# The shared expert's down product moved from the end of the expert loop into its turns, and the second norm's vectors loaded as single rows

## The reference, cut to what matters

```
for i in range(2):
    tok, q_mem = fox_mix(...) if i % 2 == 0 else rwkv7_mix(...)
    mixed = concatenate([tok, memory_cross_attention(q_mem, ...)]) @ w_out[i]
    x = layer_norm(DEEPNORM_ALPHA * x + mixed, ln1_g[i], ln1_b[i])
    ffn = moe_ffn(x, ...)
    x = layer_norm(DEEPNORM_ALPHA * x + ffn, ln2_g[i], ln2_b[i])

def moe_ffn(x2, ...):
    # for each token and each of its 6 experts e, weighted with its gate:
    #   acc[token] += gate * ((silu(x @ w_gate[e]) * (x @ w_up[e])) @ w_down[e])
    shared = (silu(x2 @ w_sh_gate) * (x2 @ w_sh_up)) @ w_sh_down
    return acc + shared
```

## Time and profile before

| | |
|---|---|
| median of 3 runs | 1965.85 us (1964.68 to 1968.91) |
| the profiled execution | 1966.91 us, its span 1965.2 us |
| busy: PE, DVE, ACT, POOL | 1791.4, 753.3, 379.9, 354.6 us |
| granted TensorE clock, mean | 0.977 |
| traffic | 541.80 MB, mean 276 GB/s over the span |
| expert loops, by the slices of the page | about 390 to 890 us and 1400 to 1918 us |

### The profile page before, as it was taken

How to read it: one execution, slowest core, us unless ns; L and a number is a source line. 1 busy time by engine, 2 the same in 40 slices (tenths; PEclk the granted TensorE clock), 3 DMA queues, 4 the chain that set the end, 5 groups by cost and what they waited for, 6 DMA issues and landing times. The chain is left out here.

```text
span 1965.2 us, 36205 instructions
## 1 busy us (share of the span) xinstructions
PE 1791.4 (91%) x12636; PEld 1111.3 (57%) x12637; DVE 753.3 (38%) x2180; ACT 379.9 (19%) x870; POOL 354.6 (18%) x450
## 2 busy tenths in 40 slices
PE   9999999889999989879999979999879999997877
PEld 7888445456666555543344458754446666664442
DVE  4222754633333223225255653416523333332225
ACT  2111651011111111102365143201001111110001
POOL 8442000011111111110022722100111111111110
PEclk9999999999999999999999979899999999999999
DMA  6220225599999999998123220207898999999997
GB/s 228 79 80 23 97 97 210 223 412 420 422 420 422 421 421 421 421 420 329 57 62 78 63 42 3 87 1 295 327 407 368 421 421 421 420 421 422 422 415 309
DMA packets 144184, 541.80 MB, mean 276 GB/s; under 512 B 31030, under 2 KB 68498, under 8 KB 94302
## 3 DMA queue, kind: packets, MB, share of 16 engines
q1 hardware_dynamic: 122782, 490.20, 62.4%
q0 software_dynamic: 21312, 50.37, 6.6%
HBM read 521.58 MB, written 46.14 MB: 289 GB/s over the span
## 5 line engine op out<-in xcount | busy, mean ns | idle before, releaser
L718 PE MATMUL bank<-W,XT 128*64 128x256 f32 x2880 | 327.0, 383 | 37.8 <-DMA W<-in_w_exp_up_dram 17.5
L718 PEld LDWEIGHTS bank<-W,XT 128*64 128x64 f32 x2880 | 234.2, 138 | 140.7 <-DMA W<-in_w_exp_gate_dram 26.2
L755 PE MATMUL bank<-W,ht 128*64 128x512 f32 x720 | 167.5, 607 | 14.0 <-DMA W<-in_w_exp_down_dram 8.6
L2260 PE MATMUL bank<-XT,room 128*128 128x512 f32 x352 | 158.7, 605 | 0.0
L729 DVE TENSOR_TENSOR sig<-sig,bank 128x256 f32<-128x256 f32 x72 | 30.4, 422 | 270.6 <-ACT sig L725 270.5
L718 PE MATMUL bank<-room,XT 128*64 128x256 f32 x864 | 103.2, 392 | 18.0 <-issue 9.7
L731 DVE TENSOR_TENSOR h<-sig,bank 128x256 f32<-128x256 f32 x72 | 30.4, 422 | 217.4 <-PE bank L718 217.4
L2260 PEld LDWEIGHTS bank<-XT,room 128*128 128x128 f32 x352 | 66.3, 193 | 82.2 <-issue 81.9
L784 POOL DMA_INDIRECT y_rows<-y,row x36 | 36.8, 1021 | 419.9 <-DVE y L777 419.9
L784 POOL DMA_INDIRECT y_rows<-XT,row x36 | 36.4, 1012 | 420.2 <-DVE XT L777 420.2
L704 ACT ACTIVATE XT<-bank 128x512 f32<-128x512 f32 x74 | 44.2, 597 | 334.8 <-PE bank L696 334.8
(11 more groups left out here) (491 smaller groups left out, 2781.3 us busy)
## 6 DMA issues: line engine op xcount, KB each, us to landing
W<-in_w_exp_gate_dram SPq DMA_DIRECT2D x88, 1024.0 KB, 25.2
W<-in_w_exp_up_dram SPq DMA_DIRECT2D x88, 1024.0 KB, 27.3
W<-in_w_exp_down_dram SPq DMA_DIRECT2D x88, 1024.0 KB, 26.8
room<-in_w_exp_gate_dram SPq DMA_DIRECT2D x40, 1024.0 KB, 22.8
third_high<-in_w_exp_down_dram SPq DMA_DIRECT2D x40, 1024.0 KB, 24.7
W<-y_rows SPq DMA_DIRECT2D x24, 1024.0 KB, 13.2
third_up<-in_w_exp_up_dram SPq DMA_DIRECT2D x20, 1024.0 KB, 25.9
w_shg<-in_w_exp_up_dram SPq DMA_DIRECT2D x20, 1024.0 KB, 22.9
```

What stands on the lines that cost most here:

```text
L718: last = pe.matmul((gate, up)[m][64 * a:64 * a + 64, :], xt[s][:, k, 64 * a:64 * a + 64], weights(w, a, m)[:, k * FE:(k + 1) * FE], start= ...
L755: last = pe.matmul(B[5 + half][64 * a:64 * a + 64, :], ht[:, j, 64 * a:64 * a + 64], weights(w, a, 2)[:, at:at + 512], start=(j == 0), sto ...
L2260: last = pe.matmul(main(i)[:], wc[i % WBUFS][:, kb, :], K.XT[:, kb, :], start=(kb == 0), stop=(kb == KD - 1))
```

## The change

The product of the shared expert's hidden part with `w_sh_down` is cut into 16 units: one tile of 128 tokens by 256 columns each. 15 of them are made in the last 15 turns of the loop, one at the start of each turn; the last is made in the ending. ACT, at the end of a turn, copies the hidden columns of the coming unit into `staged_hidden` (times 1, or times 0 in turns in which no unit is due) and makes a factor of ALPHA or 1; TensorE multiplies ahead of the choice of the slot (`shared_product`), into the bank that the up products use; DVE adds it to x (`add_shared`), and with it ALPHA is applied, so that the four multiplications at the end go. `w_sh_down` is loaded at the loop's start into a buffer of its own. y gets one buffer instead of two, and h takes the place of `sig`. The vectors of the norm are loaded as one row each and spread over the partitions by four matmuls with a row of ones, which ACT copies to SBUF. Some constants are carved out of the weights' room, and masks get smaller.

```diff
+UNITS = 16
+UNIT = NT * D // UNITS
...
+    K.upto = carve(P, F32)
+    K.heads = sb("heads", [P, P], BF16)
+    K.head_cols = sb("head_cols", [P, 2])
+    K.masks3 = sb("masks3", [P, 3 * P], BF16)
+    K.level = carve(7 * P, BF16).rearrange("p (l t) -> p l t", l=7)
+    K.due = sb("due", [P, MAX_PASSES - UNITS], BF16)
...
-                step.inc(dve.tensor_copy(K.plan_turns[:], gsum[0:1, 0, :]))
+                step.inc(dve.tensor_copy(K.plan_turns[:, 0:1], gsum[0:1, 0, :]))
+                step.inc(dve.tensor_scalar(K.plan_turns[:, 1:2], gsum[0:1, 0, :], -1.0, float(MAX_PASSES // 2), ALU.mult, ALU.add))
...
-        y = [xt_room[:, 0:D], sb("y1", [P, D])[:]]
+        y = xt_room[:, 0:D]
         turned_gates = sb("turned_gates", [P, 2, NT, ROW_PAIRS])
-        sig, h = sb("sig", [P, FE]), sb("h", [P, FE])
+        h = sb("h", [P, FE])
         ht = sb("ht", [P, 2, P])
         high = sb("third_high", [P, 2, KD * FE])
         third = [[K.room[:, 0, :], K.room[:, 1, :]], [shared.gate[:], shared.high[:]], [high[:, 0, :], high[:, 1, :]]]
         stored = [sem("stored0"), sem("stored1")]
+        sh_down = sb("w_sh_down_kept", [P, 2 * D])
+        staged_hidden = sb("staged_hidden", [P, 2, P])
...
+            before = eng.value_load(K.plan_turns[0:1, 1:2], min_val=0, max_val=MAX_PASSES // 2 - UNITS)
             for u in range(2):
-                body(u, u)
+                body(u, u, 0, before)
             turns = eng.value_load(K.plan_turns[0:1, 0:1], min_val=PAIRS // 2, max_val=MAX_PASSES // 2)
             with eng.Fori(1, turns) as turn:
                 for u in range(2):
-                    body(turn * 2 + u, u)
+                    body(turn * 2 + u, u, turn, before)
+
+        FIRST_DUE = UNITS - (MAX_PASSES // 2 - UNITS + 1) % UNITS
+
+        def unit_bits(turn, before, bits):
+            return (before + (turn + FIRST_DUE)) & bits
+
+        def stage_hidden(act, turn, before):
+            wait_from(act, shared_added, turn)
+            act.activation(due[:], K.due[:, bass.ds((before + (turn + 1)) & 63, 1)], ACT.Copy).then_inc(due_kept, 1)
+            act.wait_ge(due_kept, turn + 1)
+            act.activation(factor[:], due[:], ACT.Copy, bias=1.0, scale=ALPHA - 1.0)
+            at = unit_bits(turn + 1, before, UNITS - D // UNIT) * (P * UNIT // D)
+            act.activation(staged_hidden[:], shared.hidden[:, :, bass.ds(at, P)], ACT.Copy, scale=due[:, 0:1]).then_inc(hidden_staged, 1)
+
+        def shared_product(pe, n, turn, before):
+            pe.wait_ge(shared.loaded, 16)
+            pe.wait_ge(hidden_staged, turn)
+            pe.wait_ge(hidden_done, n)
+            at = unit_bits(turn, before, D // UNIT - 1) * UNIT
+            for j in range(2):
+                last = pe.matmul(up, staged_hidden[:, j, :], shared.w[:, j, bass.ds(at, UNIT)], start=(j == 0), stop=(j == 1))
+            last.then_inc(shared_made, 1)
+
+        def add_shared(dve, turn, before):
+            dve.wait_ge(shared_made, turn)
+            x = X_flat[:, bass.ds(unit_bits(turn, before, UNITS - 1) * UNIT, UNIT)]
+            dve.scalar_tensor_tensor(x, x, factor[:], up, ALU.mult, ALU.add).then_inc(shared_added, 1)
...
+                if m == 1 and s == 0 and not isinstance(n, int):
+                    pe.wait_ge(shared_added, shared_turn)
...
-            wait_from(eng, stored[s], through(n - 2, s))
+            wait_from(eng, stored[1 - s], through(n - 1, 1 - s))
             eng.wait_ge(down_done, 2 * n + 1 + half)
-            dst = y[s][:, half * 512:half * 512 + 512]
+            dst = y[:, half * 512:half * 512 + 512]
...
                     load_expert(K, sp, L, third_pair[a], 2, a, 2, third)
+                shared.load_down(sp, sh_down[:])
...
+                    if u == 0 and not early:
+                        shared_product(pe, n, shared_turn, before)
                     slot = None if early and n == 0 else entry(pe, K.plan_slot, n, WSLOTS - 1)
                     turn = 0 if early else entry(pe, K.plan_turn, n, PAIRS // WSLOTS)
...
+                    if u == 1:
+                        stage_hidden(act, turn, before)
...
+                    if u == 0 and not isinstance(n, int):
+                        add_shared(dve, turn, before)
...
+        self.ln.ready = (self.vectors_kept, 4)
...
-        self.shared.load_down(sp, self.down_room)
-        self.ln.load(sp)
+        for i, src in enumerate(self.ln.src):
+            sp.dma_start(self.vector_rows[:, i * D:(i + 1) * D], src).then_inc(self.ln.loaded, 16)
...
-                pe.matmul(B[2 * t + half][:], shared.hidden[:, j, t * P:(t + 1) * P], shared.w[:, j, half * 512:(half + 1) * 512],
-                          start=(j == 0), stop=False)
...
+    def shared_rest(self, pe):
         pe.wait_ge(self.shared.loaded, 16)
+        for j in range(2):
+            last = pe.matmul(self.K.banks[7][:, 0:UNIT], self.shared.hidden[:, j, T - P:T], self.shared.w[:, j, D - UNIT:D],
+                             start=(j == 0), stop=(j == 1))
+        last.then_inc(self.rest_made, 1)
+
+    def products(self, pe, y_a, y_d, passes):
+        self.shared_rest(pe)
         for t in range(2):
-            self.shared_product(pe, t)
             self.row_product(pe, t, 0)
             self.row_product(pe, t, 1)
-        pe.wait_ge(self.scaled, 1)
+        for y_kept in (y_a, y_d):
+            pe.wait_ge(y_kept, 1)
+            pe.wait_ge(y_kept, passes)
+        pe.wait_ge(self.rest_added, 1)
+        self.spread_vectors(pe)
         self.row_product(pe, 0, 2)
         self.row_product(pe, 1, 2)
-        self.shared_product(pe, 2)
-        self.row_product(pe, 2, 0)
-        self.row_product(pe, 2, 1)
-        self.row_product(pe, 2, 2)
-        self.shared_product(pe, 3)
+        pe.wait_ge(self.vectors_kept, 4)
+        for q in range(ROW_PAIRS):
+            self.row_product(pe, 2, q)
         self.turn(pe, 0)
         for q in range(ROW_PAIRS):
             self.row_product(pe, 3, q)
         for t in range(1, NT):
             self.turn(pe, t)
 
+    def spread_vectors(self, pe):
+        K = self.K
+        pe.wait_ge(self.ln.loaded, 32)
+        for i in range(4):
+            pe.matmul(K.banks[4 + i][:], K.ident[0:1, 0:1].to_broadcast([1, P]), self.vector_rows[:, i * 512:(i + 1) * 512],
+                      start=True, stop=True).then_inc(self.vectors_spread, 1)
+
+    def keep_vectors(self, act):
+        for i in range(4):
+            act.wait_ge(self.vectors_spread, i + 1)
+            act.activation(self.vectors[:, i * 512:(i + 1) * 512], self.K.banks[4 + i][:], ACT.Copy).then_inc(self.vectors_kept, 1)
...
+        dve.wait_ge(self.rest_made, 1)
+        x = X[:, NT - 1, D - UNIT:D]
+        dve.scalar_tensor_tensor(x, x, ALPHA, B[7][:, 0:UNIT], ALU.mult, ALU.add).then_inc(self.rest_added, 1)
+        dve.wait_ge(self.rest_added, 1)
         for t in range(NT):
-            dve.tensor_scalar_mul(X[:, t, :], X[:, t, :], ALPHA).then_inc(self.scaled, 1)
-        for t in range(NT):
-            dve.wait_ge(self.scaled, t + 1)
...
+            if n == 2 * ROW_PAIRS - 1:
+                self.keep_vectors(act)
```

More of the change, by code:

```diff
@@ L837, in _, with one_pass @@
                 gather(pool, 1, 1)
-                def one_pass(n, u):
+                def one_pass(n, u, turn, before):
                     read = held(pool, 2 * (n + 1))
@@ L901, in _ @@
                 pe.wait_ge(xt_a, held(pe, turns * 2 + 1))
-                ending.products(pe)
+                ending.products(pe, y_a, y_d, held(pe, turns * 2))
             @block.scalar
@@ L1094, in __init__ @@
         self.done = scope.sem(f"{name}_done")
+        self.ready = None
     def load(self, eng):
```

68 lines of the change are left out of this document (36 added, 32 removed).

## The result

The changed kernel takes 1994.99 us (median of 4 runs, 1988.3 to 1998.16), the kernel before 1966.8 us in the same comparison: a ratio of 1.0143, 95% interval 1.0119 to 1.0167. It is slower, and 25.6 us above the forecast of 1969.4. The profiled execution took 1997.32 us, its span is 1995.6 us, 30.4 more than before.

The account below looks back on a forecast made before the run. TensorE was taken to bound each loop's first half and the queue of weights the second. Loops 13.1 us later less 9.6 from the endings gave +3.5 us on 1965.85, so 1969.4 us, range 1960 to 1977.

Parts of the forecast that it names:

- Later tolls fall where TensorE waits for weights anyway: Late part of the expert loops: delays at turn starts there cost nothing more; the loops end 13.1 us later in all.
- the rival with 0.05: Both loops: TensorE is the bound in full, about 13 tolls in layer 1 and 8 in layer 0, 2002 us; chance 0.05.
- Toll: 0.1 + 2.1 = 2.2 us a turn: Each turn's start: 0.1 us until the staging is ready, 2.1 for TensorE's 20 instructions behind it; bounds 0.9 and 2.9.
- The sequencer still runs ahead: Turn's start: TensorE's sequencer is not held by the wait for staging; toll 1.0 us, 1961.6 us in all; chance 0.25.
- Reserves: Weight queue in the loops: work left at a refill, 1.4 us near 475 and 11.8 at 1696.43; only lateness beyond delays weights.
- the one at 1696.43: Layer 1, turn 10 refill: 11.8 us of queued work; TensorE 21.1 us later, so the weights shift by 9.3.
- The refill of 1504: Layer 1, turn 3 refill of weights, issued at 1504.26: 5.7 us later, with no reserve.
- The 4.79 us of the earlier trace: Layer 1, turn 2: a gap of unexplained issue time, for which a toll of 2.7 us was taken (2.2 to 3.7).
- A gain of 4.8 us: Layer 1's ending: last down weights to last sum pair takes 36 us instead of 40.8; range 3.3 to 6.5.
- twice 4.8 is 9.6: Both layers' endings: layer 0 has the same form as layer 1, so together they give back 9.6 us.
- The single y buffer waits for its scatter: Turn's end on ACT: keeping y waits 1 us for the scatter, toll 3.2 us, 1979.4 us in all; chance 0.13.
- the ending gives nothing: Endings: the last scatter sets them as before, so no gain; +13.1 us, 1979 us in all; chance 0.09.

Follow-up runs that it names:

- e4: The changed kernel with TensorE's two table reads done twice at each turn's start, behind the wait for the staging: 2099.62 us, ratio 1.0695.
- e1: The changed kernel with ACT staging the hidden block ahead of keeping y instead of behind it: 1969.85 us, ratio 1.0033 to the kernel before.
- e5: The changed kernel with the shared product moved behind the choice of the slot, into the turn's first pass: 1968.91 us, ratio 1.0018 to the kernel before.
- b5: e1 with vectors by two broadcast loads, the gates turned behind the last pass, and 16 fewer TensorE instructions ahead of the loop: 1966.79 us, ratio 1.0013.
- e3: The changed kernel with TensorE's two table reads ahead of the shared product instead of behind it: 1972.47 us, ratio 1.0045 to the kernel before.
- e2: The changed kernel with a turn's shared product cut from 256 to 8 columns, so most of the shared expert is missing: 2039.82 us.
- p1: The kernel before with 16 transposes of x done twice at the start, shifting TensorE's later code by 64 instructions: 1976.66 us, ratio 1.0057.
- c1: The kernel before with only the norm's vectors loaded as single rows and spread by TensorE: 1966.14 us, ratio 1.0006.
- b1: The changed kernel with all 16 shared products back in the ending, early load of their weights kept, vectors by broadcast loads: 1964.45 us, ratio 1.0009.
- b2: e5 with the norm's vectors by two broadcast loads instead of TensorE's spreading: 1965.56 us, ratio 1.0005 to the kernel before.
- c2: The kernel before with only y's two buffers made one: 1966.42 us, ratio 1.0006.

## Why the prediction was wrong, point by point

- **"Later tolls fall where TensorE waits for weights anyway"** is the step that failed. It set no budget. Layer 0 had 33.5 us of waits for weights to hide tolls in; 17 tolls of the forecast 2.2 are 37.4, more than these. 17 tolls of 3.07 are 52 us; with 1.0 for the later start and some 4 more for the gap at turn 2, which this execution of before did not have, that is 57, less 33.5 is 23.7; seen were 21.8 + 1.0. In layer 1, which had gaps at turns 1 and 2 before too, 15 tolls of 3.0 and 3.5 for those two turns are 48.5; less the 28.4 us of waits that went, that is 20, and 13.4 were seen. So the budget is good to some 7 us a loop. The changed kernel's trace has 0.5 us of waits for weights left, and e4 pays each added toll in full. TensorE was the bound in both loops: the rival with 0.05, whose formula (46 less 9.6) gave 2002. The formula counted fewer tolls (21) at the smaller price, so that it came near is partly luck. The step is right where the tolls are small: in e1, e5 and b5 TensorE waits for weights late in the loops again (13 to 23 us), and b5's loop in layer 0 takes no longer than before with a product in each turn.
- **"Toll: 0.1 + 2.1 = 2.2 us a turn"**: the mechanism is right (e1, e3, e4), the size is not. The price of an instruction is 0.149, near DVE's 0.14 and not the 0.105, which lay below even the 0.11 read from TensorE's own stretch; 3.07 stands above the upper bound of 2.9. That the product lies under the toll is right (e2); it takes 1.0 us and not 0.9, since eight wide records in 3.70 us are 0.46 each and not 0.44. "The sequencer still runs ahead" is refuted; its toll of 1.0 is what e1 makes of it (1.18). The rule of the Trainium skill (Perfetto Trace Analysis, Sequencer-only Instruction), that the sequencer itself stands through the wait of such an instruction, was borne out: with the wait met in time the distance fell from 3.07 to 1.18 us (e1), and with the wait behind the branches to nothing (e5).
- **Reserves**: the one at 1696.43 was exhausted as forecast (refill 24.8 us later relative to the loop's start, against 21.1; 7.4 us to landing; DMA idle). The refill of 1504 came 3.7 us later (forecast 5.7), since turn 2 in layer 1 cost 0.8 us more than before and not 2.7; between the two refills the larger toll added 21.1, where seven tolls of 2.2 would be 15.4.
- **What was missing**: code. The 4.79 us of the earlier trace rows were called unexplained. By p1 and b5 such gaps come and go with the place of the code, and such a one now stands in layer 0 too. It is worth 6.6 us (p1) to 9.9 (b5, with its other edits), the lower clock behind it taken in; e1's and e5's loops are 9.7 and 10.4 us longer with it. No run takes it out of the changed kernel by itself.
- **"A gain of 4.8 us", "twice 4.8 is 9.6"**: seen 7.6 and 1.2, sum 8.8. The sum came near, but by luck: one ending gave much more than forecast and the other much less, and the reason was right only in part. The old ending was TensorE's, 40.6 us of work in a row (c1, b1), not the transfers'. In the old ending spreading the vectors costs 3.3 us (c1); in the new one leaving it out brought nothing that can be told (b2). Layer 1's early rows were issued only at 1946.14, where E is 1946.35; in layer 0 they were issued 4.3 us ahead of E, and that ending is the shorter one.
- **"The single y buffer waits for its scatter"** is refuted (c2, and ACT's wait of 3.01 us for TensorE in the changed kernel), **"the ending gives nothing"** too, by the sum. The edits priced at nothing (constants, masks, ALPHA) were not measured by themselves.

No version beat the kernel before: b1, b2, b5, c1 and c2 can't be told from it, and e5 hardly. The product in the loop does shorten both endings (34.0 to 39.2 us in layer 0 and 36.7 to 39.5 in layer 1, before 41.6 and 40.8), but the loops take it back. Left open: why the unchanged stretch from layer 0's ending to layer 1's loop took from 4.4 us less (e3) to 5.5 us more (b5) than before, and what makes the gaps of layer 1 come and go (c2 has before's instructions on TensorE and had no gap at turn 2 there in its one profile, so the place of the code does not decide it alone; such a gap would fit the 1955 to 1971 us over which single runs of before scatter).

## What to carry to other kernels

Ahead of a wait on the engine's own sequencer count what stands behind it: all of it leaves the cover of the work before. Either have the awaited thing ready earlier (one line on ACT gave back some 22 us) or put the wait behind the table reads and branches. When a delay is said to fall into slack, sum the slack and the delays; if the delays are larger, the engine is the bound and the rest is paid in full. Time lost in the first turns of a loop may have to do with where the code lies: look for transfers of the kind "instruction" beside the gap, and shift the code, before blaming the edit.

## What the runs showed of the hardware

- TensorE's sequencer took 0.149 us for each of eight added table-read instructions (e4), 0.149 on average for 20 (the changed kernel), and gave back 0.186 for each of eight taken out from behind the wait (e3).
- Behind gaps of 2.4 us with one small product (e4), or of 1.8 us with almost none (e2), the clock stood at 1.2 GHz for 3 to 7 us in most turns; behind 1.3 us with a product of 1.1 us (the changed kernel) it stayed at 2.4 GHz from turn 3 on in all turns but one. Two kernels lost 18 us in one loop and 64 us in all to it.
- In every ending in which TensorE spread the vectors by matmuls with a single row of weights (looked at in the changed kernel, c1, e1, e5), the clock fell to 1.2 GHz at the end of them or just behind, for 3 to 7 us, in c1 with no wait of TensorE ahead. It did not fall in the endings of the kernel before and of b2, which have no such matmuls.
- In the first turns of a loop TensorE stood still for 1.5 to 6.8 us at a time, with instruction transfers of 16 KB beside it. 64 instructions more, far ahead of the loop, moved these gaps; the kernel so shifted was slower by 0.57%, of which 1.9 us passed ahead of the first loop.
